# Gates and branch outputs as four Strassen stages with weights moving, merged corners transposed on TensorE

## The reference

```python
h = rmsnorm(x, attn_norm_g)
u_b, u_c, u_x, q, k, v, g_conv, g_attn = split(h @ w_in)
y_conv = (u_b * short_conv(u_c * u_x, conv_w)) @ w_conv_out
y_attn = sliding_window_attention(q, k, v, sinks, rel_bias) @ w_attn_out
mixed = sigmoid(g_conv) * y_conv + sigmoid(g_attn) * y_attn
x = x + mixed @ w_o
x = x + square(relu(rmsnorm(x, mlp_norm_g) @ w_up)) @ w_down
out = rmsnorm(x, final_norm_g)
```

## Time and profile before

| | us |
|---|---|
| median of three runs (lowest, highest) | 763.15 (762.93, 763.7) |
| span of the profiled execution, first to last instruction | 761.7 |
| PE busy / DVE / ACT / POOL | 752.7 / 637.4 / 407.6 / 75.9 |

### The profile page before, as it was taken

The page is one execution under the profiler, slowest core; times in us unless marked ns, Lnnn a source line. Parts: engine busy times, 40 slices in busy tenths (PEclk is TensorE's granted clock), DMA queues, the critical chain, the costliest instruction groups (busy, mean ns, idle before and its releaser), DMA issues.

```text
span 761.7 us, 11518 instructions
## 1 busy us (share of the span) xinstructions
PE 752.7 (99%) x4563; PEld 675.0 (89%) x4563; DVE 637.4 (84%) x752; ACT 407.6 (54%) x529; POOL 75.9 (10%) x113
## 2 busy tenths in 40 slices
PE   8999999999999999999999999999999999999996
PEld 7888888888888999999988899889998999899985
DVE  5766688889896979886869899998799869986997
ACT  7424554453644655636616786654555356445565
POOL 3201000101112001010010101010101000010102
PEclk9999999999999999999999999999999999999999
DMA  7727313131219876779736866777676767777702
GB/s 255 244 83 278 111 55 111 56 111 55 72 39 262 242 186 169 194 237 327 235 80 198 219 160 173 174 205 177 175 209 172 215 166 190 196 184 203 194 1 111
DMA packets 70451, 128.13 MB, mean 168 GB/s; under 512 B 2620, under 2 KB 26244, under 8 KB 70404
## 3 DMA queue, kind: packets, MB, share of 16 engines
q1 hardware_dynamic: 53040, 85.23, 33.8%
q0 software_dynamic: 17152, 41.96, 25.4%
q10 hardware_dynamic: 212, 0.28, 0.1%
HBM read 121.14 MB, written 6.32 MB: 167 GB/s over the span
## 4 chain that ended last, share of the span: by engine, by line
PE 97%; DVE 1%; DMA 1%; ACT 0%; issue 0%; SPq 0%; ACTq 0%; DVEq 0%
PE pair L848 37%; PE pair L875 24%; PE pair L651 10%; PE pair L653 10%; PE pair L652 10%; PE pair L698 2%; PE pair L673 1%; PE pair L672 1%; PE pair L682 1%; DMA xn<-in_x 1%; PE pair L744 1%; PE pair L746 0%; PE pair L745 0%; PE pair L800 0%; DVE home_lo L1698 0%
## 5 line engine op out<-in xcount | busy, mean ns | idle before, releaser
L1164 ACT ACTIVATE high<-home_raw 128x2048 fp32r<-128x2048 f32 x84 | 160.9, 1916 | 156.2 <-PE pair L848 88.7
L1698 DVE TENSOR_TENSOR home_lo<-home_raw,high 128x2048 fp32r<-128x2048 f32 x84 | 192.2, 2288 | 35.3 <-ACT high L1164 34.7
L651 PE MATMUL pair<-h,wgt 128*128 128x512 f32 x320 | 126.7, 396 | 0.0
L653 PE MATMUL pair<-h,wgt 128*128 128x512 f32 x320 | 124.9, 390 | 0.0
L652 PE MATMUL pair<-h,wgt 128*128 128x512 f32 x320 | 124.8, 390 | 0.0
L653 PEld LDWEIGHTS pair<-h,wgt 128*128 128x128 f32 x320 | 60.1, 188 | 13.0
L652 PEld LDWEIGHTS pair<-h,wgt 128*128 128x128 f32 x320 | 60.3, 188 | 11.5
L651 PEld LDWEIGHTS pair<-h,wgt 128*128 128x128 f32 x320 | 60.2, 188 | 11.5
L875 PE MATMUL pair<-high,s_hi_tile 128*128 128x512 f32 x280 | 70.1, 391 | 0.0
L875 PE MATMUL pair<-home_lo,s_hi_tile 128*128 128x512 f32 x280 | 69.7, 390 | 0.0
L875 PE MATMUL pair<-high,s_lo_tile 128*128 128x512 f32 x280 | 69.7, 389 | 0.0
(11 more groups left out here) (222 smaller groups left out, 1151.8 us busy)
## 6 DMA issues: line engine op xcount, KB each, us to landing
raw<-in_w_in SPq DMA_DIRECT2D x42, 512.0 KB, 4.8
home_raw<-in_w_up SPq DMA_DIRECT2D x16, 1024.0 KB, 5.5
home_raw<-in_w_down SPq DMA_DIRECT2D x16, 1024.0 KB, 5.1
home_raw<-in_w_up POOLq DMA_DIRECT2D x12, 1024.0 KB, 8.4
home_raw<-in_w_down POOLq DMA_DIRECT2D x12, 1024.0 KB, 8.5
home_raw<-in_w_conv_out SPq DMA_DIRECT2D x4, 1024.0 KB, 8.2
home_raw<-in_w_attn_out SPq DMA_DIRECT2D x4, 1024.0 KB, 5.2
home_raw<-in_w_in SPq DMA_DIRECT2D x4, 1024.0 KB, 5.4
```

Of the source, the lines that this page charges most:

```text
L651: mm(bank[j][:, :], wh, rhs[:, 0, k, :], start=(k == 0), stop=False)
L653: last = mm(bank[j][:, :], wl, rhs[:, 0, k, :], start=False, stop=(k == KT - 1))
L1164: a(high[n % 2][:, :], home_raw[home_of(s, name)][:, :], ACT.Copy).then_inc(m_hi, 1)
L1698: v.tensor_tensor(home_lo[home][:, :], home_raw[home][:, :], f32(high[n % 2][:, :]), ALU.subtract).then_inc(m_lo, 1)
```

## The change

The four gate strips go. Ahead of w_o there are now four stages, all of the form `product` (weights moving, tokens on partitions): GC (g_conv), GA (g_attn), CO (w_conv_out), AO (w_attn_out); WO is w_o, so there are 13 stages. GC and GA use the corners and sums of h, as stage 2 did. Their sigmoids (`gate`, ACT) go to `mixed` and to `gates` (in h's place); `gate_conv` and `gate_attn` multiply the branches' corners into them on DVE; the sum of the two is made corner by corner: corners 11 and 22 on POOL (`merge` there), corners 12 and 21 on DVE. The result has tokens on partitions, so PE transposes each corner (`mixed_transposes`, 8 transposes) and ACT copies it back (`mixed_copy`). WO takes the corners in swapped order (its corner 11 is the merged 22), and the output rows are stored accordingly. GC's first weights take the place of the strip's chunks in the last mixer block. The core of the diff:

```diff
@@ sync
+            wait_strip(sp, S_MIX + 9)
+            load_block(GC, 0, 0)
+            wait_strip(sp, S_MIX + 10)
+            load_block(GC, 1, 0)
+            sp.wait_ge(hs_out, 16 * 8)
+            load_sum(HS.index(M6))
             wait_strip(sp, S_OUT - 1)
+            sp.wait_ge(m_lo, 1)
+            load_block(GA, 0, 0)
+            sp.wait_ge(t_ready, 4 * (TB - 1) + 3)
+            load_sum(HS.index(M5))
+            load_block(GA, 0, 1)
+            wait_used(sp, GC, N2)
+            load_block(GC, 1, 1)
+            sp.wait_ge(pv_ready, 4 * TB)
+            load_sum(HS.index(M7))
+            sp.wait_ge(pv_out, 4 * TB)
+            load_sum(HS.index(M3))
...
@@ gpsimd
+            pool.wait_ge(hs_out, 16 * 8)
+            pool.dma_start(home_rows(home_of(GC, "T3")), weights(GC, 0, 1)).then_inc(t3_base, 16)
             for n in range(1, TB):
+                if n == 2:
+                    add_t3(GC)
                 for qd in range(QUADS if n < TB - 1 else QUADS - 1):
                     mask(n, qd)
+            def merge(at_):
+                pool.wait_ge(weighed, at_ + 1)
+                pool.wait_ge(gated, at_ + 1)
+                u = four_of(mixed, *CORNERS[at_])
+                g.tensor_tensor(u, u, attn_gate(at_), ALU.add).then_inc(mix_pool, 1)
             for s in range(STAGES):
+                if s > GC:
+                    add_t3(s)
+                if s == GC:
+                    wait_strip(pool, S_OUT - 1)
+                elif s == WO:
+                    pool.wait_ge(s_lo, part_no(AO, M7) + 1)
                 else:
                     wait_used(pool, s - 1, M7)
                 pool.dma_start(home_rows(home_of(s, "T1")), weights(s, 0, 0)).then_inc(t1_base, 16)
-                if s == 0:
+                if s == GC:
                     mask(TB - 1, QUADS - 1)
+                if s == WO:
+                    merge(1)
                 pool.wait_ge(t1_base, 16 * (s + 1))
                 pool.dma_start(home_rows(home_of(s, "T1")), weights(s, 0, 1), accum_op=ALU.add).then_inc(t1_in, 16)
+                if s == AO:
+                    merge(0)
@@ tensor
+            def mixed_transposes(at_, r):
+                i, j = CORNERS[at_]
+                pe.wait_ge(mix_pool, at_ + 1) if at_ < 2 else pe.wait_ge(mix_done, at_ - 1)
+                pe.wait_ge(mix_ready, at_) if at_ else None
+                for k in range(4):
+                    for b in range(2):
...
+                if s < WO:
...
+                    product(s, M1, True)
+                    if s == GC:
+                        values(TB - 1, 2)
+                        transpose_probs(TB - 1, 3)
+                        pe.wait_ge(logits, QUADS * TB)
...
+                    product(s, N2, True)
+                    if s == GC:
+                        values(TB - 1, 3)
+                    pe.wait_ge(copied, 3 * s + 1)
+                    product(s, M6, False)
...
+                    product(s, M5, True)
+                    pe.wait_ge(copied, 3 * s + 2)
+                    if s == AO:
+                        mixed_transposes(0, 3)
+                    product(s, M7, False)
...
+                    product(s, N4, False, between={1: mixed_corner_22} if s == AO else {})
+                    continue
+                product(s, M1, True, between={2: mixed_corner_12, 4: mixed_corner_21} if s == WO else {})
+                if s == WO:
+                    pe.wait_ge(mix_ready, 3)
...
@@ vector, in mixer_block of the last block
+                if it == TB - 1:
+                    sum_t2(GC)
+                    low_part(GC, M1)
+                else:
+                    lo_chunks(S_MIX + 3, 3, it)
@@ vector, the list
             probs_lo(3, 2)
             normalise(3, 3)
-            lo_chunks(S_OUT + 1)
+            sum_t4(GC)
+            low_part(GC, N2)
             attention_out(3, 2)
             probs_lo(3, 3)
+            low_part(GC, M6)
             attention_out(3, 3)
...
+            s_low(AO, M5)
+            sum_c11(AO)
+            low_part(AO, M5)
             gate_attn(0)
+            s_low(AO, M7)
+            low_part(AO, M7)
+            s_low(AO, M3)
+            low_part(AO, M3)
+            sum_c22(AO)
             gate_attn(1)
+            s_low(AO, N4)
+            low_part(AO, N4)
+            sum_c12(AO)
+            sum_t2(WO)
+            gate_attn(2)
+            merge(2)
+            s_low(WO, M1)
+            low_part(WO, M1)
+            gate_attn(3)
+            merge(3)
+            sum_t4(WO)
+            low_part(WO, N2)
+            s3(WO)
+            s2(WO)
+            s_low(WO, N2)
```

More of the change, by code:

```diff
@@ L92, in is_up @@
 def is_up(s):
-    return s < 3 or s % 2 == 0
+    return s > WO and s % 2 == 1
 def up_no(s):
-    return s if s < 3 else 3 + (s - 4) // 2
-PARTED = [0, 1] + list(range(3, STAGES, 2))
+    return s if s < WO else WO + (s - WO - 1) // 2
+PARTED = [CO, AO] + list(range(WO, STAGES, 2))
 def part_no(s, i):
@@ L1890, in _ @@
-            s_low(0, M5)
-            sum_c11(0)
-            low_part(0, M5)
-            s_low(0, M7)
-            low_part(0, M7)
-            s_low(0, M3)
-            s3(1)
-            low_part(0, M3)
-            s_low(0, N4)
-            sum_c22(0)
-            low_part(0, N4)
-            sum_t2(1)
-            s_low(1, M1)
-            sum_c12(0)
-            low_part(1, M1)
-            s_low(1, N2)
-            s2(1)
-            gate_conv(0)
-            sum_t4(1)
-            low_part(1, N2)
@@ L1932, in _ @@
-            low_part(2, M6)
-            sum_c11(2)
-            low_part(2, M5)
-            merge(0)
-            low_part(2, M7)
-            lo_chunks(S_OUT + 2)
-            low_part(2, M3)
-            s_low(3, M1)
-            sum_c22(2)
-            low_part(2, N4)
-            gate_attn(0)
-            sum_t2(3)
-            sum_c12(2)
-            gate_attn(1)
-            low_part(3, M1)
-            merge(1)
-            lo_chunks(S_OUT + 3)
-            s3(3)
-            merge_tile(2, 0)
@@ L1971, in _ @@
-            low_part(3, M7)
+            sum_c11(GC)
+            low_part(GC, M5)
+            low_part(GC, M7)
+            sum_t2(GA)
+            low_part(GC, M3)
+            sum_c22(GC)
+            low_part(GC, N4)
+            low_part(GA, M1)
+            sum_t4(GA)
+            sum_c12(GC)
+            low_part(GA, N2)
+            s3(CO)
+            low_part(GA, M6)
+            sum_c11(GA)
+            low_part(GA, M5)
+            low_part(GA, M7)
+            sum_t2(CO)
+            s2(CO)
@@ new lines, in _ @@
+            low_part(GA, M3)
+            s_low(CO, M1)
+            sum_c22(GA)
+            low_part(GA, N4)
+            s_low(CO, N2)
+            s1(CO)
+            low_part(CO, M1)
+            sum_c12(GA)
+            sum_t4(CO)
+            low_part(CO, N2)
+            s_low(CO, M6)
+            s4(CO)
+            low_part(CO, M6)
+            s_low(CO, M5)
+            s3(AO)
+            sum_c11(CO)
+            low_part(CO, M5)
+            gate_conv(0)
+            s_low(CO, M7)
@@ new lines, in _ @@
+            low_part(CO, M7)
+            sum_t2(AO)
+            s_low(CO, M3)
+            low_part(CO, M3)
+            s2(AO)
+            s_low(CO, N4)
+            sum_c22(CO)
+            low_part(CO, N4)
+            gate_conv(1)
+            s_low(AO, M1)
+            sum_c12(CO)
+            low_part(AO, M1)
+            gate_conv(2)
+            s_low(AO, N2)
+            gate_conv(3)
+            sum_t4(AO)
+            low_part(AO, N2)
+            s_low(AO, M6)
+            s1(AO)
@@ L1984, in _ @@
-            sum_t4(4)
-            drain_n4(3, 1)
+            low_part(WO, M3)
+            s_low(WO, M3)
+            drain(WO, 4, 1, 1, M7, ALU.subtract)
+            low_part(WO, N4)
+            s_low(WO, N4)
+            sum_t2(WO + 1)
+            drain(WO, 5, 0, 1, M3, ALU.add)
+            low_part(WO + 1, M1)
+            drain_n4(WO, 0)
+            sum_t4(WO + 1)
+            drain_n4(WO, 1)
             h2_low(N2)
-            low_part(4, N2)
+            low_part(WO + 1, N2)
             h2_s3_s2()
```

767 lines of the change are left out of this document (336 added, 431 removed).

## The result

| | before | after |
|---|---|---|
| median, us (lowest, highest) | 763.2 (762.93, 763.7) | 789.57 (788.14, 790.44) |
| span of the profiled execution | 761.7 | 788.5 |

The change makes the kernel 3.4% slower, ratio 1.0342, interval [1.0328, 1.0357]: 26.4 us, where I had forecast 6.9 slower and 777 as the upper end.

What follows compares the result with a forecast made beforehand. TensorE, busy 99% of the span, was taken to bound the kernel. 763.15 - 8.6 (its work) + 7.4 (first stage) + 1.3 (clock) + 2.2 (merge(0)) + 4.6 (border) = 770.0 us, range 758 to 777.

Steps and rivals of the forecast that it cites:

- PE's own work: Whole kernel: 164.5 us of TensorE work removed, 155.9 added, so its work falls by 8.6 us to 754.5.
- The first stage: GC: TensorE waits for T1 ahead of its fourth product, M5, 7.4 us (4.8 to 16.4).
- the landing: GC: T1's accumulating transfer, issued from 245.8, takes 10.9 us beside 4 MB of other loads and lands at 256.7.
- The clock: M5 in GC: after the wait TensorE restarts at 1.2 GHz, costing 1.3 us (bounds nothing and 5.4).
- merge(0), 5.3 taken with a wait of 2.2: AO: GpSimd's sum takes 5.3 us, priced from L621, so TensorE waits 2.2 ahead of corner 11's transposes.
- 6 if the DVE operations beside it hold it back for their own time: AO: upper bound, in us, of TensorE's wait for merge(0) ahead of corner 11.
- rival D: POOL and DVE in each other's way, both merges stretched by 4 us, T1 at 15.6: 775 to 781, chance 0.14.
- it ends CO's last gate product 2.7 us in: Entry to AO: DVE finishes CO's last gate product 2.7 us in, so gate_attn(0) ends at 18.5.
- The border: AO to WO: TensorE waits 4.6 us in w_o's N2 for DVE's s_low (bounds 2 and 7).
- DVE's 25.3 against PE's 20.7: AO to WO, from M7's end: DVE needs 25.3 us through s_low N2; PE reaches N2's second kind after 20.7.
- merge(1) is inside this: AO to WO: merge(1) adds nothing to the 4.6 wait; DVE's 2.5 and POOL's 5.3 against PE's 7.3.
- DVE's 36.8 against 38.1 in CO: CO: DVE's 9 large and 15 small operations take 36.8 us against PE's 38.1.

Runs made afterwards that it cites:

- e11: e9 plus sum_c12(GC) on VectorE ahead of sum_t2(GA) and ScalarE's high part of w_o's M5 ahead of its s_high: 761.08 us, ratio 0.9971 to the kernel before.
- e10: Changed kernel with sum_c11(GC) moved ahead of low_part(GC, M6) on VectorE, beside the last mask: 790.19 us, ratio 1.0352.
- e7: e6 with e8's border order, GA's B11 and B12 loads behind M3's sums, and sum_t2(GA) behind sum_c22(GC): 766.54 us, ratio 1.0048.
- e1: Changed kernel with T1's base and accumulating load issued on GpSimd ahead of the last mask: 779.4 us, ratio 1.0207.
- e3: Changed kernel with 40 useless matmuls filling TensorE's wait for T1 ahead of M5: 788.45 us, ratio 1.0338.
- e4: Changed kernel with sum_t2(AO) moved behind low_part(CO, M3) and s2(AO) on VectorE: 786.47 us, ratio 1.0304.
- e8: Changed kernel with VectorE's w_o border reordered to s3, s_low(N2), s2, low_part(N2): 789.02 us, ratio 1.0338.
- e9: e7 with VectorE's order mended at the last mask, sum_t2(GA) and the border, corner 21 transposed earlier, ScalarE's M6 high part first: 763.4 us, ratio 1.001.
- e2: Changed kernel with both GpSimd sums of merged corners, merge(0) and merge(1), moved to VectorE: 780.44 us, ratio 1.0224.
- e5: Changed kernel with VectorE made to wait behind gate_attn(0) until GpSimd has written merge(0): 782.29 us, ratio 1.0245.
- e6: Changed kernel with the edits of e1, e2 and e4 together: 766.83 us, ratio 1.0057.

## Why the prediction was wrong

The sign and the places were right, the sizes were not: 763.15 became 789.57 in place of 770.0, outside the range.

- **PE's own work, -8.6: right in pace, short by the stops.** A product takes 5.44 wherever nothing waits. But e11, with 3.4 us of idle, has a span only 2.3 under the kernel before, so 2.9 are missing. A stop costs more than its idle row: in e11 the group at 404.05 plus its 1.81 plus the 0.22 of idle ahead of the next would be 406.08, and the next starts at 406.37. That is the 0.3 a stop found above; seven stops make 2.1 of the 2.9, and the rest is not placed. My sum had no term for such borders.
- **The first stage, 7.4 taken, 4.8 to 16.4 allowed: 11.2 (1.61 + 9.61), 11.5 with the small wait of 0.32 in N2.** The failed term is the landing: I took 10.9, near the median of twelve transfers, while counting 4 MB of traffic beside it; it took 13.9. e10 shows that the issue didn't set its end; that the traffic did is read from the stretches and fits e7, whose transfer took 8.4. The mask, taken at 0.63, took 2.62 beside low_part(M6), but e10 shows that this cost nothing.
- **The clock, 1.3: 6.7.** I priced one place of the three; M5's 2.2 lay inside my bounds, and the 2.9 and 1.6 hang on waits that I had as 2.2 and 4.6, without a term for the clock behind them. The 1.6 belongs to the profiled execution: e1, e3 and e4 have that wait without it.
- **merge(0), 5.3 taken with a wait of 2.2: 8.78 with a wait of 7.17.** This step failed most. I had the mechanism as an upper bound ("6 if the DVE operations beside it hold it back for their own time") and as a part of rival D, and then took the mean of the earlier trace rows, which was itself half held. By the lock the sum was there to be worked out: DVE's four operations beside it, 6.75 us, and POOL's own 2.4. I also set aside the Trainium skill's 2.2 us ("GPSIMD Engine Reference", Performance versus the Vector engine) because L621 spoke against it; with DVE held the sum took 2.38, so the estimate from the page is near POOL's own time.
- **What came before it: gate_attn(0) ended 21.2 us into AO, not 18.5.** The step that failed is the entry, "it ends CO's last gate product 2.7 us in": it ended 5.5 in (370.4 against 364.93), and from there DVE took 15.7 where I had counted 15.8. DVE had waited 3.05 us in CO for T3's accumulation, which no step of mine followed; without that wait, in e4, the entry was still 4.9 (368.77 against 363.86), so most of it is DVE's own work.
- **The border, 4.6 taken, 2 to 7 allowed: 6.0** (1.46 + 0.68 + 1.37 + 2.48), and 1.6 of slow clock. DVE's 25.3 against PE's 20.7 was the right comparison, and short by one item: DVE ended s_low(WO, N2) 27.7 after M7 (431.98 against 404.30), which is about 25.3 and the 2.2 that merge(1) took from low_part. So "merge(1) is inside this" was wrong in kind. e8's order gained nothing here; e9's, with merge(1) on DVE, left less.
- **No term at all: 1.5.** PE waited 1.01 in CO's N4 and 0.48 in AO's N2, both for DVE; I had DVE's 36.8 against 38.1 in CO as fitting, and didn't follow its wait for T3. e4 removed 1.3 of the 1.5.
- **Rival D** (each other's way, T1 at the crowded end) was what happened, and more; I gave it 0.14 and 775 to 781. Its stretch of 4 us over 5.3 was about right for merge(0), 3.5; the late entry, the clock and the restarts, which it lacked too, put the time above its range.

## What to carry to other kernels

Work moved to GpSimd beside a busy VectorE is not free and not slow by a ratio: it can wait for VectorE's whole run of SBUF operations (four at merge(0), two at L621, one at merge(1)), so price it between its own time and that run plus its own time, or place it where VectorE reads PSUM. When a row that carries a price is a group, open it: a mean of 2.67 us was 1.31 and 4.04, and the difference was the mechanism. A wait of PE can carry a second price, the clock behind it: here the waits of 2.44 us and more mostly did, for 1.4 to 3.0 us, and it differed between executions, so it is no evidence for an edit made elsewhere. A single change of order on an engine near its limit gained 0 to 3 us here (e10, e8, e4) and moved what it didn't gain; work taken off the contended pair of engines gained 9.

## What the runs showed of the hardware

- POOL's addition of 128x1024 float32 takes 2.38 us with DVE held, 8.78 beside four DVE operations from SBUF, and makes a DVE operation of 2.28 last 4.48 when it gets in first.
- POOL's product of 128x512 takes 1.31 us beside DVE operations with one operand in PSUM, and 4.04 beside two from SBUF.
- An idle time of PE of 1.37 to 1.79 us left the next group of eight at 2.06 to 2.14; one of 2.44 was followed by a group of 3.49. Behind one of 2.45 to 2.49, always in the same place, three of eight profiled executions lost 0.1 us (e1, e3, e4) and five lost 1.6 to 1.8 (the changed kernel, e2, e5, e6, e10). In e10 the granted clock was still 1.00 from 432 to 433, with PE at work again since 431.97, and 0.50 from 434 to 436: it fell after the wait was over. Waits of 7.2 to 11.3 us cost 1.4 to 3.0. No row of this case shows what decides it.
- An accumulating load of 1 MB landed in 8.4 us where the loads beside it were moved away and in 13.9 and 15.3 where they weren't.
